# Rotary rotation by transfers, a norm factor on GpSimd, later sigmoids and two barriers fewer in a two-block kernel

## The reference, cut to what matters

```python
def rope(t, positions):                      # queries and keys of retention
    t1, t2 = t[..., : d // 2], t[..., d // 2:]
    return jnp.concatenate([t1 * cos - t2 * sin, t1 * sin + t2 * cos], axis=-1)

yr = (yr - mu) * lax.rsqrt(var + 1e-5) * ret_gn_g
yr = jax.nn.silu(rg) * yr
yg = gated_delta_chunked(gq, gk, gv, log_a, beta)
yg = yg * lax.rsqrt(jnp.mean(yg * yg, axis=-1, keepdims=True) + NORM_EPS) * gdn_norm_g
yg = jax.nn.silu(gz) * yg
merged = jax.nn.sigmoid(gate_a) * yr + jax.nn.sigmoid(gate_b) * yg
```

## Time and profile before

| what | value |
|---|---|
| median of three runs | 2975.98 us (2973.90 to 2976.29) |
| the profiled execution's own time | 2973.03 us |
| its span, first to last instruction | 2971.3 us |
| mean granted TensorE clock | 0.998 of full speed |
| busy: TensorE products / weight loads | 99% / 85% of the span |
| busy: VectorE / ScalarE / GpSimd | 65% / 49% / 1% |
| DMA queue of SyncE | 498.21 MB, 45.3% of 16 engines' span |

### The profile page before, as it was taken

How to read it: one execution, slowest core, us unless ns; L and a number is a source line. 1 busy time by engine, 2 the same in 40 slices (tenths; PEclk the granted TensorE clock), 3 DMA queues, 4 the chain that set the end, 5 groups by cost and what they waited for, 6 DMA issues and landing times.

```text
span 2971.3 us, 39706 instructions
## 1 busy us (share of the span) xinstructions
PE 2933.0 (99%) x16274; PEld 2517.8 (85%) x16274; DVE 1934.6 (65%) x2473; ACT 1453.6 (49%) x1850; POOL 30.0 (1%) x61
## 2 busy tenths in 40 slices
PE   8999999999999999999999999999999999999998
PEld 8899888888888878788888888888888888888887
DVE  7645567678656568777778775457567555655555
ACT  5434644356444356566656663444336334444434
POOL 0000200000000000000000000000000000000000
PEclk9999999999999999999999999999999999999999
DMA  6544345565444533333333344544344455444453
GB/s 260 192 172 156 142 175 194 189 234 181 170 182 172 184 145 142 114 128 128 126 131 127 126 145 164 192 183 170 143 171 190 190 198 198 183 186 188 182 197 142
DMA packets 72373, 504.73 MB, mean 170 GB/s; under 512 B 8160, under 2 KB 8288, under 8 KB 12416
## 3 DMA queue, kind: packets, MB, share of 16 engines
q1 hardware_dynamic: 71568, 498.21, 45.3%
q0 software_dynamic: 336, 3.80, 0.3%
q10 hardware_dynamic: 288, 0.18, 0.0%
HBM read 500.06 MB, written 2.10 MB: 169 GB/s over the span
## 4 chain that ended last, share of the span: by engine, by line
PE 94%; DVE 2%; ACT 2%; issue 1%; DMA 1%; SPq 0%; ACTq 0%; DVEq 0%
PE double L1268 84%; PE bank L1268 9%; PE bank L1271 1%; DMA raw<-in_wall 0%; ACT whi L1640 0%; DVE wlo L1989 0%; DMA vec<-in_vec 0%; ACT L1675 0%; DVE cacc L1995 0%; DVE acc L1989 0%; DVE AA L1995 0%; SPq L2738 0%; ACT L1835 0%; DVE cst L2012 0%; ACT AA L1779 0%
## 5 line engine op out<-in xcount | busy, mean ns | idle before, releaser
L1268 PE MATMUL double<-AA,whi 128*128 128x512 f32 (+1 forms) x5008 | 1657.4, 383 | 6.6 <-DVE wlo L1989 4.3
L1268 PE MATMUL double<-AA,wlo 128*128 128x256 f32 (+1 forms) x4624 | 1300.0, 281 | 0.0
L1640 ACT ACTIVATE whi<-raw 128x1024 fp32r<-128x1024 f32 x926 | 925.0, 1048 | 736.7 <-PE double L1268 700.5
L1989 DVE TENSOR_TENSOR wlo<-raw,whi 128x1024 fp32r<-128x1024 f32 (+1 forms) x934 | 1102.9, 1214 | 231.1 <-ACT whi L1640 228.7
L1268 PEld LDWEIGHTS double<-AA,whi 128*128 128x128 f32 x5008 | 917.3, 188 | 197.9 <-DVE wlo L1989 6.8
L1268 PEld LDWEIGHTS double<-AA,wlo 128*128 128x128 f32 x4624 | 871.8, 189 | 1.4
L1268 PE MATMUL double<-whi,AA 128*128 128x512 f32 x1536 | 496.2, 396 | 0.5 <-DVE wlo L1989 0.5
L1268 PEld LDWEIGHTS double<-whi,AA 128*128 128x128 f32 x1536 | 288.5, 188 | 63.1 <-DVE wlo L1989 2.3
L1268 PE MATMUL double<-whi,BB 128*128 128x512 f32 x1024 | 317.0, 389 | 0.0
L1268 PE MATMUL double<-wlo,AA 128*128 128x512 f32 x768 | 299.2, 390 | 0.0
L1268 PEld LDWEIGHTS double<-whi,BB 128*128 128x128 f32 x1024 | 192.2, 188 | 40.4
(11 more groups left out here) (343 smaller groups left out, 1980.3 us busy)
## 6 DMA issues: line engine op xcount, KB each, us to landing
raw<-in_wall SPq DMA_DIRECT2D x462, 1024.0 KB, 4.8
raw<-in_wall SPq DMA_DIRECT2D x9, 256.0 KB, 6.5
X<-in_xT SPq DMA_DIRECT2D x1, 2048.0 KB, 11.4
Mm<-in_memT POOLq DMA_DIRECT2D x1, 2048.0 KB, 15.8
mblk<-in_memT SPq DMA_DIRECT2D x8, 256.0 KB, 5.6
out<-XT SPq DMA_DIRECT2D x8, 256.0 KB, 2.9
dec<-in_dec POOLq DMA_DIRECT2D x1, 1536.0 KB, 9.0
hs<-in_hsT SPq DMA_DIRECT2D x4, 272.0 KB, 5.7
```

The costliest lines, as they stand in the source:

```text
L1268: return q.matmul(out, lhsT, rhs, start=start, stop=stop, skip_group_check=True)
L1640: q.activation(whi[j % SPL][:, c], raw[j % RAW][:, c], ACT.Copy).then_inc(S("w_hi"), 1)
L1989: return q.tensor_tensor(out, a, b, o)
```

## The change

- The constant `rot` and the TensorE step of `rope` are gone. When `rq` or `rk` has been read, GpSimd issues two transfers from partitions 64 to 127 of `rqk` to partitions 0 to 63 of a temporary and the other way round (step `rshift`, 128 KB each). The sign goes into the sine. VectorE's three operations stay; the first reads the temporary in place of a bank. The temporary is held from the read to the rope, and no side bank is taken.
- The delta rule's factor: ScalarE's logarithm and exponential at the end of `g_nrm` are replaced by two GpSimd instructions on 128 x 4, a multiply-add and a power of -0.5; `g_end` waits for those.
- The sigmoids of `rg`, `gta`, `gz` and `gtb` become a step of their own (`..._sig`), added by `g_gate` in the slot after the read, behind the older tasks' steps of that slot. What comes after the gate's product starts one slot earlier; for the last `rtr` one slot is put in.
- `r0` is put right behind the splits of unit 4, and the read of `u` 1 moves from unit 5, second half, to unit 4, second half.
- The two `drain()` calls in front of the attention heads and behind `mk` are removed; the attention heads begin two slots later in the list of tasks.

```diff
-    "rot": 1.0 * (p == f - 64) - 1.0 * (p == f + 64),
+    "room": np.zeros((P, P)), "mhalf": np.full((P, 4), -0.5), "sgn": np.where(np.arange(P) < 64, -1.0, 1.0)[:, None],
...
+    lo_to(10)
+    r = at["r0s", 0]
+    add("r0", 0, b=r["b"], full=r["full"], a=up("nrm_act", 2), r=up("nrm_vec", 4))
+    side.free(r["b"], "nrm_vec", at["r0", 0]["r"] - 3)
+
     def first_rows():
-        r = at["r0s", 0]
-        add("r0", 0, b=r["b"], full=r["full"], a=up("nrm_act", 2), r=up("nrm_vec", 4))
-        side.free(r["b"], "nrm_vec", at["r0", 0]["r"] - 3)
         evac("u", 0, first[0], 3, pool=up("pooled"))
...
-    hooks = {(4, 0): first_rows, (5, 1): second_read, (6, 0): load_rest}
+    hooks = {(4, 0): first_rows, (4, 1): second_read, (6, 0): load_rest}
...
     def g_heads():
         live, h, slots = [], 0, 0
+        yield
+        yield
         while h < 8 or live:
...
-    drain()
     tasks.append(g_heads())
...
-            r = evac(stage, h, bs, full, t=ts, tf=(a[1], b[1]), sig=up("sig", 2))
-            tasks.append(g_gate(stage, h, ts, then))
+            r = evac(stage, h, bs, full, t=ts, tf=(a[1], b[1]))
+            tasks.append(g_gate(stage, h, r, then))
...
-    def g_gate(stage, h, ts, then):
+    def g_gate(stage, h, r, then):
+        ts = r["t"]
+        add(stage + "_sig", h, t=ts, tf=r["tf"], ev=r["ev"], sig=up("sig", 2))
         yield
         r = add(stage + "_in", h, t=ts, g=up("gated", 2))
         tmp.free(ts[0], "gated", r["g"] - 1)
         tmp.free(ts[1], "gated", r["g"])
-        yield
         if then:
             tasks.append(then(h))
+        yield
+
+    def ev_rqk(n):
+        def f(tag, h, bs, full):
+            r = evac(tag, h, bs, full)
+            t, tf = tmp.take()
+            tmp.held.add(t)
+            add("rshift", (h, n), t=t, tf=tf, s=32 * (h + 1))
+            return emptied(r)
+        return f
...
     def g_ret(h):
         for n in range(2):
-            b, bf = side.take()
-            t, tf = tmp.take()
-            r = add("rope", (h, n), b=b, bf=bf, t=t, tf=tf, full=up("ret_pe"), v=up("ret_vec", 3))
-            side.free(b, "ret_vec", r["v"] - 2)
-            tmp.free(t, "ret_vec", r["v"])
+            m = at["rshift", (h, n)]
+            r = add("rope", (h, n), t=m["t"], s=m["s"], v=up("ret_vec", 3))
+            tmp.free(m["t"], "ret_vec", r["v"])
...
         add("rgt", h, v=up("ret_vec", 4))
         yield
+        if h == 3:
+            yield
...
-        r = add("g_nrm", h, t=t, tf=tf, a=up("gdn_act", 6))
-        tmp.free(t, "gdn_act", r["a"] - 2)
+        r = add("g_nrm", h, t=t, tf=tf, a=up("gdn_act", 4), p=up("gdn_pool", 2))
+        tmp.free(t, "gdn_act", r["a"])
...
         pair("T", "mk", phase4, ev_plain("mk"), half=True)
-    drain()
...
-        def s_rope(key, r):
-            h, n = key
-            free(r["bf"])
-            q.wait_ge(S("ev"), at[("rq", "rk")[n], h]["ev"])
-            mm_group(bank[r["b"]][:, :], C("rot"), f2(rqk[h % 2][n])).then_inc(S("ret_pe"), 1)
...
-            q.wait_ge(S("gdn_act"), r["a"] - 2)
-            rsqrt(ors[:, :], osum[:, :], 1.0 / 128, C("eps6"), "gdn_act", r["a"])
...
         def s_rope(key, r):
             h, n = key
-            free(r["tf"])
-            q.wait_ge(S("ev"), at[("rq", "rk")[n], h]["ev"])
-            q.wait_ge(S("ret_pe"), r["full"])
             x3 = two(tmps[r["t"]][:, :])
-            tt(x3, two(bank[r["b"]][:, :]), s2, ALU.mult).then_inc(S("ret_vec"), 1)
+            q.wait_ge(S(f"rshift{n}"), r["s"])
+            if h:
+                q.wait_ge(S("ret_pe"), at["rsc", (h - 1, 1)]["full"])
+            tt(x3, x3, s2, ALU.mult).then_inc(S("ret_vec"), 1)
...
         def s_g_end(h, r):
-            q.wait_ge(S("gdn_act"), at["g_nrm", h]["a"])
+            q.wait_ge(S("gdn_pool"), at["g_nrm", h]["p"])
...
+            elif stage == "rshift":
+                h, n = key
+                free(r["tf"])
+                q.wait_ge(S("ev"), at[("rq", "rk")[n], h]["ev"])
+                x, y = f2(rqk[h % 2][n]), tmps[r["t"]]
+                if h:
+                    q.wait_ge(S("ret_vec"), at["rope", (h - 1, n)]["v"])
+                q.dma_start(y[0:64, :], x[64:128, :]).then_inc(S(f"rshift{n}"), 16)
+                q.dma_start(y[64:128, :], x[0:64, :]).then_inc(S(f"rshift{n}"), 16)
+            elif stage == "g_nrm":
+                q.wait_ge(S("gdn_act"), r["a"])
+                if key:
+                    q.wait_ge(S("gdn_vec"), at["g_end", key - 1]["v"])
+                q.tensor_scalar(ors[:, :], osum[:, :], 1.0 / 128, 1e-6, ALU.mult, ALU.add).then_inc(S("gdn_pool"), 1)
+                q.wait_ge(S("gdn_pool"), r["p"] - 1)
+                q.tensor_tensor(ors[:, :], ors[:, :], C("mhalf"), ALU.pow).then_inc(S("gdn_pool"), 1)
```

More of the change, by code:

```diff
@@ L118, in constants @@
         "ltc": (p <= f) & same, "su": (p > f) & same, "strict": (f < p) & same,
-        "eye": p % 64 == f[:, 0:64], "rot": 1.0 * (p == f - 64) - 1.0 * (p == f + 64),
+        "eye": p % 64 == f[:, 0:64], "room": np.zeros((P, P)), "mhalf": np.full((P, 4), -0.5), "sgn": np.where(np.arange(P) < 64, -1.0, 1.0)[:, None],
         "invf": (1.0 / (np.float32(10000.0) ** (np.arange(0, 128, 2, dtype=np.float32) / np.float32(128))))[
@@ L713, in make_plan @@
         if h == 0:
-            turns("T", (("rq", ev_plain("rq")), ("rk", ev_plain("rk"))), phase3, half=True, hooks=hooks3)
+            turns("T", (("rq", ev_rqk(0)), ("rk", ev_rqk(1))), phase3, half=True, hooks=hooks3)
         else:
-            pair("T", "rq", phase3, ev_plain("rq"))
-            pair("T", "rk", phase3, ev_plain("rk"))
+            pair("T", "rq", phase3, ev_rqk(0))
+            pair("T", "rk", phase3, ev_rqk(1))
         pair("N", "rv", phase3, ev_rv)
@@ L1167, in program @@
     cacc_r = place(kpos[1], [P_, 512], F32R, name="cacc_r")
-    ones_r = place(con_off + 4 * CON["rot"][0], [P_, P_], F32R, name="ones_r")
+    ones_r = place(con_off + 4 * CON["room"][0], [P_, P_], F32R, name="ones_r")
     mblk = [place(kpos[n], [P_, 512], name=f"mblk{n}") for n in (0, 1, 5, 6, 3, 4, 2, 7)]
@@ L1613, in tensor_program @@
         own = {"xt": s_xt, "r0s": s_r0s, "mix": s_mix, "vtr": s_vtr, "att_z": s_att_z, "att_e": s_att_e, "att_o": s_att_o, "fin": s_fin,
-               "mixf": s_mixf, "gab1": s_gab1, "gab2": s_gab2, "rope": s_rope, "rsc": s_rsc, "rav": s_rav, "rtr": s_rtr,
+               "mixf": s_mixf, "gab1": s_gab1, "gab2": s_gab2, "rsc": s_rsc, "rav": s_rav, "rtr": s_rtr,
                "cvn": s_cvn, "g_dec": s_g_dec, "g_mat": s_g_mat, "g_inv0": s_g_inv0, "g_up": s_g_up, "g_down": s_g_down,
@@ L1784, in s_trig @@
                 q.wait_ge(S("trig_vec"), r["v"])
-                q.activation((sinb if n == 1 else cosb)[:, :], ang[:, :], ACT.Sin).then_inc(S("trig_act"), 1)
+                if n == 1:
+                    q.activation(sinb[:, :], ang[:, :], ACT.Sin, scale=C("sgn")).then_inc(S("trig_act"), 1)
+                else:
+                    q.activation(cosb[:, :], ang[:, :], ACT.Sin).then_inc(S("trig_act"), 1)
         def s_gab1(_, r):
@@ L1971, in scalar_program @@
                "a3": gained("a3", lambda k: g12[:, k:k + 1]), "a5": gained("a5", lambda k: V("norm_x_g_2", k)),
[L1972 to L1974 removed]
+               "a7": gained("a7", lambda k: V("norm_ffn_g_2", k)), "trig": s_trig, "gab1": s_gab1, "gab2": s_gab2, "rg_sig": token_sigmoid(lambda h, m: Gt[h % 2][:, m, :]),
+               "gta_sig": token_sigmoid(None), "rtr": s_rtr, "rav": s_rav, "begin_gdn": s_begin_gdn, "cvs": s_cvs, "cvq": s_cvq, "cvn": s_cvn,
+               "gz_sig": token_sigmoid(lambda h, m: gz[m][:, :]), "gtb_sig": token_sigmoid(None), "g_dec": s_g_dec, "g_inv0": s_g_inv0, "g_up": s_g_up, "g_down": s_g_down,
                "g_w": s_g_w, "g_nrm": s_g_nrm, "memn": s_memn, "mv": s_mv, "a4": s_a4, "x_s": s_x_s,
@@ L2319, in f @@
                     q.wait_ge(S("ret_vec"), at["rope", (h - 2, n)]["v"])
+                    q.wait_ge(S(f"rshift{n}"), at["rshift", (h - 2, n)]["s"])
                 full(r)
```

10 lines of the change are left out of this document (6 added, 4 removed).

## The result

The changed kernel takes 2951.7 us (median of 4 runs, 2949.5 to 2952.8) against 2975.1 us of the kernel before in the same measurement: a ratio of 0.9920 with a 95% interval of 0.9903 to 0.9938. Measured once more with the last experiments it was 0.9922 (0.9910 to 0.9935). The profiled spans tell the same, 2971.3 us before and 2947.7 us after.

The account below looks back on a forecast made before the run. TensorE bounds the kernel, busy 2933.0 of 2971.3 us. Terms 6.9 + 2.3 + 1.0 + 4.2 + 1.6 + 1.0 + 0.6 - 1.2 = 16.4 us gave 2959.6 us; 8-in-10 range 2954 to 2968 us.

Parts of the forecast that it names:

- Rotation: Retention heads: rotation products leave TensorE, 1.72 us a head, 6.9 us for four; transfers hide in a 20 us window.
- Start: Start of the kernel: TensorE's wait for the read of `u` 1 (`ub`) goes, 2.3 us, bounds 0 to 2.3.
- Barriers: Drain before the gates: the `vst` wait goes, 1.0 us; the drain behind `mk` is worth nothing.
- Last retention transposes: TensorE's longest stall, on `yn`, goes because `rgt` runs ahead of `gab1`: 4.2 us.
- Norm factor: Delta rule: factor on GpSimd removes stalls on `Tn` in head 0, 1.6 us, and `ob` in head 7, 1.0 us.
- Idle time of VectorE before `ob`: Sign listed as showing the forecast wrong: VectorE standing idle before `ob`; no size given.
- Sigmoids: Gate sigmoids put last: 0.6 us won for `gz` at 1665.8 us, 1.2 us lost for `gtb` in head 7.
- A: Rival: closed stalls reopen at the next late operation; rotation, start and barrier gains stay, 2966 us; chance 0.20.
- B: Rival: the factor's two GpSimd steps are slow, gains eaten at 7.7 us; at 10 us 2985 us; chance 0.03.
- C: Rival: rotation transfers land beyond the 20 us window; at 30 us four heads lose 10 us each, 3000 us; chance 0.02.
- D: Rival: gate and norm parts do nothing and reordering costs 5 us; 5 us left, 2971 us; chance 0.08.
- the 16 that were named: Sign expected in the profile after: ScalarE with 16 fewer table loads, at L1675 and L1677.

Follow-up runs that it names:

- dose: Changed kernel plus seven artificial TensorE stalls (1 to 12 GpSimd memsets each) in the last feed-forward phase; span 2980.9 us in one run.
- i1: Changed kernel with normalisation hooks half a unit later and the last gtb sigmoid ahead of the end of its step; 2948.23 us, ratio 0.9909.
- p_sig: Kernel before with only the sigmoid steps (rg, gta, gz, gtb) moved to the end of their unit; 2971.23 us against 2975.85, ratio 0.9984.
- p_rot: Kernel before with only the rotation by two transfers and signed sine in place of the product with `rot`; 2968.58 us, ratio 0.9977.

## Why the prediction fell short, step by step

- **Rotation, 6.9 us forecast, 5.1 measured.** The place, the price of 1.72 us a head, the hidden transfers and the free window held. The step that failed is the overlap: the sentence that what stands behind the rope "comes sooner, not later" missed that TensorE comes sooner still. The scores now wait for `rr` in every head, which costs 1.1 us in head 0 and 0.3 us in each of the others, 2.0 us in all.
- **Start, 2.3 forecast, 4.1 measured.** The stall went in full. The term, with 2.3 us as its upper bound, lacked 1.8 us behind it, which the waits do not show: half clock, and likely the 0.3 us that every stall of dose costs beyond its row. That the profile of before had half clock there is luck in part, as three of eight such profiles have none.
- **Barriers, 1.0 forecast, 1.1 measured** for `vst`, and the second worth nothing, as said. Missed: the changed pace at 596 to 695 us, 1.9 us, which the forecast had at nothing, and which no row that it read could have priced.
- **Last retention transposes, 4.2 forecast, 5.1 measured**: the stall in full, 1.6 us behind it in the same way, less 0.7 us in the stretch up to 1136 us, whose cause was not looked for.
- **Norm factor, 1.6 and 1.0 forecast, 1.7 and 1.9 measured.** Right in both places; 0.7 of the 1.9 us is pace again. GpSimd's price was mis-sized, 1.6 us for 0.4, without effect on TensorE. Idle time of VectorE before `ob` had been named as a sign of being wrong; it stood there 1.51 us, and only the slack behind it saved the term.
- **Sigmoids, +0.6 and -1.2 forecast, +4.6 and -1.3 measured.** This is the step that failed most. The forecast booked the one `Tn` wait that its row showed as 0.57 us and did not ask where else ScalarE had sigmoids between a read and `Tn`. The same wait stood there four times: 1.98 us at 1155.8 us, hidden in the row "issue", and 0.8 us by the k-th product in each of heads 2, 4 and 6. The loss at `gtb` came out at its size, but that is luck in part: `Tc`, the place named, lost 0.5 us, and 0.7 us came at `AA`, which the forecast had not named, likely because the normalisation of the memory tokens now shares ScalarE with the late sigmoids.

The surplus in the table is thus 4.0 us of `Tn` waits, 3.5 us behind the two long stalls, 2.6 us of pace and 0.4 us of small ends at `vst`, `Tn` and `ob`, less 1.8 us at the rotation, 0.7 us behind the transposes and under 0.1 us at `Tc` and `AA`: 8.0 us. 0.5 us of it is lost outside the stretches of the table, 0.3 of them in the first 44 us: 16.4 + 8.0 - 0.5 = 23.9 us.

Of the rivals, A (the stalls move) came true in three places, `rr`, `AA` and `Tc`, together 3.2 us and not the 6 us it priced. B fell: two steps of together 1.6 us are far from 7.7. C fell: 2.2 us against a window of 20. D fell: every part but the second barrier shows. ScalarE's table loads fell from 35 to 27 at each of two lines, the 16 that were named. TensorE's busy time came to 2920.8 us where 2926 were named: the forecast had counted the products taken away, and not what half clock and pace add to the busy time of the others.

The Trainium skill, "TensorE: Matmul & The Clock Gate", section "Why this matters for your kernels", warns against idle gaps of TensorE between bursts of products, since the clock then falls back to its lower level. The trace agrees, and already for gaps shorter than the page names: half clock followed each of the 13 placed gaps of 2.4 us and more, and the kernel's own gaps of 2.0 us in 8 of 13 cases.

## What to carry to other kernels

Price a stall of TensorE of 2 us or more with the clock behind it: read the granted clock in the windows after each, and add about half of the time that TensorE works at half clock (1.5 us at the shorter stalls here, 2.5 us at the longest). Where one engine has a wait in front of work that is already ready, look for every instance of that pattern and not only for those whose wait has a name; "issue" with a long single member is one of them. And where a product is taken away, the next thing that TensorE reaches early is the first place to look for a new wait.

## What was not expected of the hardware

- A stall of 2.4 us came with 3.4 us, one of 4.7 with 6.8 and one of 7.1 with 10.2 us at half clock. In the longer ones the stretch began 2.0 and 4.9 us before the stall's end, and only what lay behind the end cost time; the longest cost 9.8 us in all.
- The kernel's own stalls of 2.0 to 2.6 us have it or not from one execution to the next, and now and then such a stretch begins where no stall above 1.5 us stands in front of it (1202.8 us in i1, 1126.2 and 1221.7 us in p_sig, 1752.0 us in p_rot). What decides there stays open.
- The same pairs of products run at 353 or 347 ns for 100 us at a time, at full clock and without waits; removing a barrier 340 us earlier switched it, and so did the removed wait for `ob` for the 40 us behind it. The cause stays open.
- A power on GpSimd takes 1.0 us for 128 x 4 elements while VectorE stands still and 1.4 us when it starts beside a VectorE product. A multiply-add of the same size takes 0.19 us, and 1.23 us beside VectorE's split, which itself lasts 1.22 us.
